# Clearing the accumulators with four matmuls per feed-forward stage, dropping a tiny matmul after fp32 work, and giving the first hidden tile another buffer

## The reference

```python
# first block: h + 0.5*ffn, h + mixer, h + 0.5*ffn, twice
def swiglu(h, w_gate, w_up, w_down):            # d_ff = 2816, four times
    return (silu(h @ w_gate) * (h @ w_up)) @ w_down
# mixers: s5_mixer (a state space scan), moba_mixer (causal attention, 8 heads)
# second block: two attention mixers (ab: 8 + 8 heads; mla: 16 heads), each followed by
h = h + square(relu(rms(h) @ w1)) @ w2          # d_ff = 4096, twice
```

## Time and profile before

| | |
|---|---|
| time, median of 3 runs | 1672.29 us (1665.34 to 1675.03) |
| the profiled execution | 1672.29 us, span 1670.5 us |
| PE busy, mean granted clock | 1586.9 us (95% of the span), 0.965 |
| DVE, ACT, POOL busy | 1089.4, 760.8, 462.9 us |
| matmuls | 13069 |

### The profile page before, as it was taken

How to read it: one execution, slowest core, us unless ns; L and a number is a source line. 1 busy time by engine, 2 the same in 40 slices (tenths; PEclk the granted TensorE clock), 3 DMA queues, 4 the chain that set the end, 5 groups by cost and what they waited for, 6 DMA issues and landing times.

```text
span 1670.5 us, 31435 instructions
## 1 busy us (share of the span) xinstructions
PE 1586.9 (95%) x13069; PEld 1517.5 (91%) x13069; DVE 1089.4 (65%) x1067; ACT 760.8 (46%) x995; POOL 462.9 (28%) x413
## 2 busy tenths in 40 slices
PE   5989998899999999999999999999999997999997
PEld 5989996699999999999889999976999996699996
DVE  7798869966556665566556555535755565476565
ACT  4434460055434543457555444645534346654432
POOL 6999617701000100017430000654100023510000
PEclk8999996699999999999999999989999998999998
DMA  6535640045555455555335554440555542045552
GB/s 219 195 126 198 217 148 15 1 152 192 187 203 187 179 205 201 194 179 177 126 109 203 196 201 176 170 146 3 185 194 176 199 163 90 26 156 215 186 199 75
DMA packets 39025, 265.96 MB, mean 159 GB/s; under 512 B 4352, under 2 KB 6400, under 8 KB 7328
## 3 DMA queue, kind: packets, MB, share of 16 engines
q1 hardware_dynamic: 37808, 261.41, 43.9%
q0 software_dynamic: 1136, 3.38, 0.7%
HBM read 263.70 MB, written 1.06 MB: 158 GB/s over the span
## 4 chain that ended last, share of the span: by engine, by line
PE 79%; DVE 12%; ACT 3%; issue 2%; POOL 2%; DMA 0%; DVEq 0%; SPq 0%; ACTq 0%; POOLq 0%
PE ps L554 73%; DVE wlo L1306 3%; PE ps L850 2%; DVE gst L1486 2%; PE ps L860 2%; DVE xlo L1312 1%; ACT whi L1000 1%; PE ps L838 1%; DVE h L1322 1%; DVE rstd L1335 1%; POOL pm L418 1%; PE ps L742 1%; DMA h<-in_xT 0%; ACT pm L1223 0%; POOL rinv L417 0%
## 5 line engine op out<-in xcount | busy, mean ns | idle before, releaser
L1306 DVE TENSOR_TENSOR wlo<-raw,whi 128x2048 fp32r<-128x2048 f32 x246 | 599.9, 2444 | 240.3 <-ACT whi L1000 240.0
L554 PE MATMUL ps<-xhi,whi 128*128 128x256 f32 x2048 | 572.9, 280 | 20.2 <-DVE xlo L1312 12.7
L1000 ACT CAST whi<-raw 128x2048 fp32r<-128x2048 f32 x246 | 469.5, 1913 | 239.3 <-PE ps L554 239.2
L554 PE MATMUL ps<-xlo,whi 128*128 128x256 f32 x2048 | 570.7, 279 | 0.0
L554 PE MATMUL ps<-xhi,wlo 128*128 128x256 f32 x2048 | 570.5, 279 | 0.0
L554 PEld LDWEIGHTS ps<-xhi,whi 128*128 128x128 f32 x2048 | 388.1, 189 | 22.3 <-issue 13.0
L554 PEld LDWEIGHTS ps<-xhi,wlo 128*128 128x128 f32 x2048 | 388.9, 190 | 0.0
L554 PEld LDWEIGHTS ps<-xlo,whi 128*128 128x128 f32 x2048 | 388.6, 190 | 0.0
L554 PE MATMUL ps<-hhi,whi 128*128 128x256 f32 x1216 | 337.7, 278 | 0.7 <-DVE hlo L1362 0.5
L554 PE MATMUL ps<-hhi,wlo 128*128 128x256 f32 x1216 | 337.2, 277 | 0.0
L554 PE MATMUL ps<-hlo,whi 128*128 128x256 f32 x1216 | 337.2, 277 | 0.0
(11 more groups left out here) (235 smaller groups left out, 2072.4 us busy)
## 6 DMA issues: line engine op xcount, KB each, us to landing
raw<-in_wstream SPq DMA_DIRECT2D x247, 1024.0 KB, 4.8
h<-in_xT SPq DMA_DIRECT2D x1, 1024.0 KB, 8.1
out_hT<-h SPq DMA_DIRECT2D x2, 512.0 KB, 3.0
biasA<-bias_rows POOLq DMA_DIRECT2D x5, 192.0 KB, 4.8
biasB<-bias_rows POOLq DMA_DIRECT2D x3, 192.0 KB, 7.1
braw<-in_s5b POOLq DMA_DIRECT2D x1, 512.0 KB, 3.9
CL<-in_s5c POOLq DMA_DIRECT2D x4, 128.0 KB, 4.4
tg<-in_tgain POOLq DMA_DIRECT2D x1, 384.0 KB, 3.5
```

Of the source, the lines that this page charges most:

```text
L554: return pe.matmul(o, l, r, start=first, stop=last, skip_group_check=True)
L1000: act.copy(whi[:, slot, :], raw[:, slot, :]).then_inc(S("whi_ready"), 1)
L1306: dve.tensor_tensor(wlo[:, slot, :], raw[:, slot, :], whi[:, slot, :], ALU.subtract)\
```

## The change

In words: (1) `settle` and `after_fp32` are gone everywhere. (2) A new `zero_acc` runs four bf16 matmuls of a 1 x 128 zero weight with 512 zero columns, with the start flag, into banks 0 to 3, once in each ffn and mlp stage; all matmuls of `down` then accumulate. In ffn it stands between `proj_first` and the up projection, in mlp behind `stats`. `zrow` grows from 64 to 512 elements, which moves what is laid out behind it by 896 bytes. (3) In mlp, PE has no written-out first pass any more: the loop starts at 0. (4) In ffn, ACT and DVE write out the first pass of the loop, as PE does, and the hidden tile of iteration 0 goes to buffer 2 instead of 0. (5) Buffer 2 moves to 2080 and 4128 bytes into `sq`, 32 bytes off the placement that `moving_at` gives.

```diff
-        hhi2 = sb("hhi2", [P, 2, T], F32R, where=sq_at + 4096)
-        hlo2 = sb("hlo2", [P, 2, T], F32R, where=sq_at + 6144)
+        hhi2 = sb("hhi2", [P, 2, T], F32R, where=sq_at + 2048 + 32)
+        hlo2 = sb("hlo2", [P, 2, T], F32R, where=sq_at + 4096 + 32)
-        zrow = sb("zrow", [1, 64], BF16)
+        zrow = sb("zrow", [1, 512], BF16)
...
-            def settle(bank):
-                mm(ps[0:32, bank, 0:64], zrow[0:1, 0:32], zrow[0:1, 0:64], True, True)
...
+            def zero_acc():
+                for b in range(4):
+                    mm(ps[:, b, :], zrow[0:1, 0:P], zrow[0:1, :], True, False)
...
-                                   hid_hi(b)[:, f, :], hid_lo(b)[:, f, :], first and f == 0 and dt % 2 == 0,
-                                   final and f == 1)
+                                   hid_hi(b)[:, f, :], hid_lo(b)[:, f, :], False, final and f == 1)
...
                 proj_first(F, 4, x_wait(k))
                 start_stage(k)
+                zero_acc()
                 proj(F + 1, None, 5)
                 stats(k)
...
-                        proj(n, i, 4 + 2 * b, after_fp32=u == 0 and i is None)
+                        proj(n, i, 4 + 2 * b)
...
-                        down(st, n + 2, u, i, u, first=u == 0 and i is None)
+                        down(st, n + 2, u, i, 2 if u == 0 and i is None else u)
...
                 stats(k)
                 start_stage(k)
-                def body(i):
+                zero_acc()
+                with pe.Fori(0, (MLP_IT - 1) // 3) as i:
                     for u in range(3):
                         n = F + 1 + 2 * u
-                        proj(n, i, 4 + (1 + u) % 3, after_fp32=u == 0 and i is None)
-                        down(st, n + 1, u, i, u, first=u == 0 and i is None)
-                body(None)
-                with pe.Fori(1, (MLP_IT - 1) // 3) as i:
-                    body(i)
+                        proj(n, i, 4 + (1 + u) % 3)
+                        down(st, n + 1, u, i, u)
...
-                hidden(st, 0, None, 0, 2, None)
-                with act.Fori(0, (FFN_IT - 1) // 2) as i:
+                hidden(st, 0, None, 2, 2, None)
+                def body(i):
...
+                body(None)
+                with act.Fori(1, (FFN_IT - 1) // 2) as i:
+                    body(i)
```

More of the change, by code:

```diff
@@ L563, in chunk_ready, with proj @@
                 pe.wait_ge(S("wlo_ready"), at_iter(n + 1, BODY, i))
-            def settle(bank):
-                mm(ps[0:32, bank, 0:64], zrow[0:1, 0:32], zrow[0:1, 0:64], True, True)
-            def proj(n, i, bank, operand=None, wait_k=None, first_k=0, stop_k=None, after_fp32=False):
+            def proj(n, i, bank, operand=None, wait_k=None, first_k=0, stop_k=None):
                 ohi, olo = operand or (xhi, xlo)
@@ L575, in proj @@
                 chunk_ready(n, i)
-                if after_fp32:
-                    settle(bank)
                 for m in range(2 if stop_k is None else 1):
@@ L599, in proj_first, with proj_tok @@
                 last.then_inc(S("w_used"), 1)
-            def proj_tok(n, bank, W, wait_k=None, after_fp32=False):
+            def proj_tok(n, bank, W, wait_k=None):
                 slot = n % NSLOT
                 chunk_ready(n, None)
-                if after_fp32:
-                    settle(bank)
                 order = [(tt, k) for k in range(KT) for tt in range(TT)] if wait_k else \
@@ L631, in stats, with down @@
                 last.then_inc(S("ss_done"), 1)
-            def down(st, n, i0, i, b, first=False, final=False):
+            def zero_acc():
+                for b in range(4):
+                    mm(ps[:, b, :], zrow[0:1, 0:P], zrow[0:1, :], True, False)
+            def down(st, n, i0, i, b, final=False):
                 chunk_ready(n, i)
@@ L713, in s5 @@
                 stats(k)
-                proj(F + 1, None, 5, after_fp32=True)
+                proj(F + 1, None, 5)
                 for f in range(4, 8):
                     turn_B(f)
-                proj(F + 2, None, 6, after_fp32=True)
+                proj(F + 2, None, 6)
                 pe.wait_ge(S("s5_bt"), 5)
@@ L726, in s5 @@
                 pe.wait_ge(S("root_ready"), roots_upto(k))
-                proj(F + 3, None, 7, after_fp32=True)
+                proj(F + 3, None, 7)
                 pe.wait_ge(S("s5_k0"), 4)
@@ L798, in project_rows @@
                 rows = TOK[st]
-                waiting, after_fp32 = [], False
+                waiting = []
                 for c in rows:
@@ L804, in project_rows @@
                     proj_tok(F + q, 4 + q % 3, c["W"] + (c["v"][1] if c["v"] and c["dst"] else 0),
-                             wait_k=x_wait(k) if q == 0 else None, after_fp32=after_fp32)
-                    after_fp32 = False
+                             wait_k=x_wait(k) if q == 0 else None)
                     if q == 0:
-                        after_fp32 = True
                         start_stage(k)
@@ L1344, in gate, with hidden @@
                     .then_inc(S("gate_scaled"), 1)
-            def hidden(st, i0, i, b, per, n_up):
+            def hidden(st, i0, i, b, per, n_up, buffer=None):
                 dve.wait_ge(S("w_used"), at_iter(n_up + 1, BODY, i))
                 swiglu = st.startswith("ffn")
+                hb = b if buffer is None else buffer
                 if i0 > 0:
@@ L1361, in hidden @@
                 dve.wait_ge(S("hidden_hi_ready"), at_iter(BEFORE[st]["hhi"] + i0 + 1, per, i))
-                dve.tensor_tensor(hid_lo(b), us[:, :, :], hid_hi(b), ALU.subtract).then_inc(S("hidden_lo_ready"), 1)
+                dve.tensor_tensor(hid_lo(hb), us[:, :, :], hid_hi(hb), ALU.subtract).then_inc(S("hidden_lo_ready"), 1)
             def acc_landed(st, n):
@@ L1373, in ffn, with body @@
                 split_lo(F + 3)
-                hidden(st, 0, None, 0, 2, F + 1)
-                with dve.Fori(0, (FFN_IT - 1) // 2) as i:
+                hidden(st, 0, None, 0, 2, F + 1, buffer=2)
+                def body(i):
                     for u in range(2):
@@ L1382, in ffn @@
                         split_lo(c + 4, i)
+                body(None)
+                with dve.Fori(1, (FFN_IT - 1) // 2) as i:
+                    body(i)
                 n = F + 3 * FFN_IT
```

## The result

On the same chip the changed kernel took 1678.67 us (median of 20 runs), the kernel before 1668.38 us (20 runs): ratio 1.0056, 95% interval 1.0035 to 1.0079, so it is slower by 0.35% to 0.8%. One run of the changed kernel took 3129 us; it is left out of the ratio, as such runs are in all that follow. The forecast was 1667.3 us and "no change". The profiled execution took 1678.76 us, span 1677.0 us, which is 6.5 us more than that of before.

The account below looks back on a forecast made before the run. PE, busy 95% of the span, was taken as the bound. Settle -2.4, clearing +3.1 in ffn and +0.6 in mlp, pace -6.3: -5.0 us from 1672.29 gives 1667.3 us, range 1662 to 1687.

Parts of the forecast that it names:

- The pace: Fp32r streams run at one of two paces, 4.4 ns apart; mlp0 turns fast, -6.3 us, mlp1 stays as it is.
- The slower side: buffer 2 in ffn: Rival, 0.20: ffn's first hidden tile, 32 bytes off, turns ffn1 to ffn3 slow, +18.4 us, 1685.7 us.
- The sign by which the prediction told a fast start: Streams whose second matmul starts 0.22 us behind the first end up fast; at 0.19 us most stay slow.
- The argument against the rival: In ffn the next projection is again on `xhi`, so the pace may return there, costing 0.2 us a stage.
- both mlp slow: Rival, 0.10: both mlp stages run slow, mlp1 losing 6.3 us, 1679.9 us.
- mlp0 gains 6.3 us: mlp0's stream no longer stalls at its first down and keeps the fast start: 1440 x 4.4 ns.
- settle removed: 0.128 us saved each, bounds 0 and 0.2; 19 in moba, ab, mla and s5 count, -2.4 us.
- The row taken for it: Timeline row going straight from fp32 to fp32r: first to second matmul 0.22 us, as behind settle; basis for 0.128 us.
- That settles in ffn are hidden: Removing settle in ffn gains nothing: PE waits at the first down, or in ffn0 for DVE, anyway.
- zero_acc in ffn: Four zero matmuls ahead of stats cost 1.03 us (0.8 to 1.25) in ffn1 to ffn3, +3.1 us; ffn0's wait covers it.
- In mlp: zero_acc behind stats replaces settle; partly covered by PE's wait at the first down: 0.31 us each, +0.6 us.
- The zero for the written-out loops: One loop in mlp, ACT and DVE written out in ffn: zero, at most 0.2 us an ffn stage either way.

Follow-up runs that it names:

- a1: The changed kernel with buffer 2 moved back by 32 bytes onto the placement; 1677.58 us, ratio 0.9966 to the kernel before.
- a2: The changed kernel with ffn's first hidden tile in buffer 0 again, buffer 2 still 32 bytes off; 1675.4 us, ratio 0.9967 to the kernel before.
- b1: The kernel before with the settle matmul left out, nothing else; 1669.12 us, ratio 0.9941.
- b3: The kernel before with buffer 2, used in mlp alone, moved 32 bytes off its placement; 1673.72 us, ratio 0.9994.
- c1: The kernel before without settle, with the four clearing matmuls and the single loop in mlp alone; 1671.16 us, ratio 0.9955.
- f2: The kernel before with the four clearing matmuls added in ffn alone, start flags kept; 1678.31 us, ratio 1.0016.
- f1: The kernel before with parts 4 and 5 of the change alone; 1676.15 us, ratio 1.0025.
- m1: The kernel before plus a test behind it: 24 turns of seven 48-matmul streams with different starts; plain starts slow 20 of 72, no time given.
- m3: The kernel before plus a test: 20 turns of streams, plain, behind settle, or at other offsets; plain starts slow 8 of 20, no time given.
- m4: The kernel before plus a test: 48 turns, one stream on the placement, one starting 32 bytes off then on it; slow 6/48 and 27/48, no time given.
- after_again: The changed kernel, nothing altered, run once more on another chip; 1680.45 us, ratio 1.0013 to the kernel before.
- d1: The kernel before, all settles out, one put ahead of the first down of each ffn and mlp stage; 1663.3 us, ratio 0.995.
- d2: d1 with the inputs of moba, ab and mla 384 bytes further; 1663.97 us, ratio 0.9929 to the kernel before.
- e1: a1 with a settle-like matmul ahead of ffn's first down and a settle behind the clearing in mlp; 1663.87 us, ratio 0.9942 to the kernel before.
- m2: The kernel before plus a test: streams with inputs at every multiple of 32 bytes, four times each, moving then stationary; 113.3 to about 120 ns, no time given.

## Why the prediction was wrong

**The step that failed** is in "The pace" and its rival "The slower side: buffer 2 in ffn". The pace was rightly called the term that decides, and that ffn's first down on the shifted buffer might turn a whole stage was written down, at 0.20. What was put in the forecast was that ffn keeps what one profile showed, three fast stages. The runs show odds in its place, and in the profiled execution ffn2 and ffn3 drew the slow pace, at +6.18 and +6.19 us. Of the restarts at the first down of an ffn stage on the placement without a settle 6 of 21 stages stayed slow (before, a1, a2, b1, b3, c1, f2), of those 32 bytes off 7 of 12 (the changed kernel three times, f1); by themselves the stage counts could differ by chance (about one in seven), and it is the streams of m1, m3 and m4 that show it: 34 of 140 against 41 of 72. So the rival was right in its mechanism and wrong in its size: it took 3 stages at 6.1 us, and the change adds 3 x (0.57 - 0.24) x 6.2 = 6.1 us on average. The sign by which the prediction told a fast start, 0.22 us from the first matmul to the second, does not tell it: its own have 0.22 us and are slow. The argument against the rival, that the next projection is on the placement again and the pace may return, came true in 43% of these streams (31 of 72). The measured 1678.67 us lies 1.2 us from the case "both mlp slow", which did not happen: that nearness is luck.

**"mlp0 gains 6.3 us"**: it gained 5.14. That a stream without a stall keeps its fast start was half true: it keeps its start, fast or slow. In the profiled execution mlp0 drew fast; in `after_again` it drew slow, and in a1 both mlp stages did. So the gain by that path was partly luck. What keeps mlp from staying slow in the changed kernel is buffer 2, which shakes a slow stream loose at its first turn; in none of the six profiled executions with it (four kernels) does an mlp stage stay slow. The same downs cost 5 x 0.23 us and a little behind each, 1.24 us a stage, which the prediction had not at all. Against odds of 0.24 for a slow stage (by the restarts alone; of the ten mlp stages without such downs or settles at the down 4 were slow) the cure is worth 2 x 0.24 x 6.2 = 3.0 us and costs 2.5.

**"settle removed", 19 x 0.128 = -2.4 us**: mis-sized. It is 0.88 - 0.54 = 0.34 us in ffn1 and 0.31 in moba's rows, above the upper bound of 0.2; the rows of moba and ab, s5, and an estimated 0.33 for mla give -4.5 us. Measured place by place, from the matmul ahead to the second behind, the 19 save 5.5 us (most of them 0.33, the first in the rows of moba and the one of mla 0.22, the first in the rows of ab 0.03, the last in s5 0.13); in ab and s5 later waits and slower streams take part of it back. The row taken for it showed the distance of the two fp32r matmuls behind the change of type, not the distance from the fp32 matmul to them, where the rest lies. The loss on the other side, 15 of 24 slow starts behind fp32, touches only short streams here. In the kernels themselves such starts on `xhi` were slow 45 times of 66 without a settle (after three times, a1, a2, b1, c1, d1, d2, e1) and 3 times of 32 with it (before, b3, f1, f2). That settles in ffn are hidden was right (-0.01 us each).

**"zero_acc in ffn", 1.03 us**: 1.17, within its bounds. The matmuls start 0.24 us apart (0.23 taken from the 512-column fp32r ones), and the way into bf16, taken as 0 with 0.2 as its bound, is 0.10. The Trainium skill, "TensorE: Matmul & The Clock Gate", section "Back-to-back issue gap", has 131 ns; for these, with a weight load each, the trace does not agree. That all of it is on the path held, in three stages of three, and so did that the wait of ffn0 covers it: its first down begins at 48.14 us, before at 48.41. **In mlp**, 0.31 us: 0.42. The zero for the written-out loops held too: from stats to the first down ffn changes by 0.01 us.

**The balance** over many executions, from these terms: settle -4.5, clearing in ffn +3.5 and in mlp +0.8, downs on buffer 2 in mlp +2.5, first downs of ffn 32 bytes off 3 x 48 x 4.9 ns = +0.7, odds in ffn +6.1, odds in mlp -3.0: +6.1 us, 0.37%. The three ratios of the changed kernel, 1.0056, 1.0013 and 1.0049, have 0.39% as their mean. This sum is an estimate, and the agreement is closer than the intervals warrant; that f1 alone costs 0.25% (its interval reaches from nothing to 0.5%) goes with its part of it, 3 x 0.24 + 6.1 + 2.5 - 3.0 = 6.3 us or 0.38%. Other runs fit less well: b1 should gain 0.27% by it and gained 0.59% (0.30 to 0.87), and a1 should be 0.38% below the changed kernel, where the ratios differ by 0.73%. Neither was run beside the changed kernel, so it is open whether the odds differ between chips or a term is missing.

**Left open.** The runs don't show what in PE makes the two paces, why settle makes the start fast, nor why it failed in mlp1 of d1 and in s5, where the projection behind the second settle was slow in three profiles of four. Nor do they show why a tile 32 bytes off frees a running stream every time and leaves a starting one slow in over half the cases. The attention of ab and mla and the end differ by 1.5 to 2.5 us between the two profiled executions, with instructions that the change doesn't touch. Such differences come without the change too. B3 and f2 run the instructions of the kernel before in these parts: from the last down of ffn3 to the first of mlp0 they are 4.1 and 2.2 us shorter than it, from the last down of mlp0 to the first of mlp1 2.0 and 1.0 us longer, and behind the last down b3 is 1.7 us shorter. What sets these was not followed up, and neither they nor ffn0 are in the balance. The differences of the parts add to 0.7 us more than the 6.5 of the whole; the rest is in stretches that weren't taken apart.

## What to carry to other kernels

Count matmuls in equal stretches before and after, in more than one execution: where a stage draws its pace at its start, one profile shows a draw, and an edit is worth its change of the odds. Keep the first tile of a long stream where streams were found fast, test one other place, and let a long stream start behind a tiny bf16 matmul where PE waits anyway (0.13 us in d1); ahead of short streams behind fp32 work it costs 0.33 us, more than the 0.2 us that 48 matmuls lose at the slow pace. A price read from the wrong pair of instructions is no bound: measure from the last instruction of the old kind to the second of the new.

## What the runs showed of the hardware

- Fp32r matmuls of 256 columns run at 113.3 or about 117.8 ns at one granted clock (1.00, the 2.4 GHz level), and keep the pace over up to 1440 matmuls. It is not the traffic of weight loads, ACT or POOL: in m1 to m4 it is there with a DMA share of 0.00 and ACT and POOL at 0.00 us busy in 700.
- The pace depends on where the input tile lies, with the weights in one place: 113.3 to 120.0 ns over offsets in steps of 32 bytes (m2); with the inputs moving it nearly repeats after 256 bytes.
- Starting 32 bytes off and going on at the placement, a stream stayed slow in 41 cases of 72; a running stream that passed through 48 matmuls 32 bytes off was fast behind them in 60 of 60.
- With one bf16 matmul of 64 columns ahead the start was fast in 44 of 44 test streams on the placement, in 29 of 32 projections on `xhi` in the kernels (before, b3, f1, f2), and in 14 of 15 stages; 32 bytes off it doesn't help (20 of 20 slow), at 128 it helps in part (12 of 20 slow, against 20 of 20 without it).
- From an fp32 matmul straight to fp32r is 0.34 us shorter than over the bf16 one, but starts slow in 15 of 24.
